# A row scale moved behind the first expert: router and gather read the residual without its norm

## The reference, cut to what matters

```
h = x * rsqrt(mean(x*x) + EPS) * g_ffn            # RMSNorm; the first factor is one number per row
logits = h @ w_router                             # 256 x 8
top_v, top_i = top_k(logits, 2); wts = softmax(top_v)
x = x + sum_e combine[:, e] * (silu(h @ w1[e]) * (h @ w3[e])) @ w2[e]
out = rmsnorm(x, g_final)
```

## Time and profile before

| | |
|---|---|
| median of three runs | 1710.83 us (1710.59 to 1711.66) |
| the profiled execution | 1712.28 us, span 1710.5 us |
| TensorE busy, share of the span | 1668.2 us, 98% |
| VectorE busy | 1283.9 us, 75% |
| ScalarE busy | 1051.2 us, 61% |
| mean granted clock of TensorE | 0.995 |
| DMA | 493.96 MB, mean 289 GB/s |

### The profile page before, as it was taken

The page is one execution under the profiler, slowest core; times in us unless marked ns, Lnnn a source line. Parts: engine busy times, 40 slices in busy tenths (PEclk is TensorE's granted clock), DMA queues, the critical chain, the costliest instruction groups (busy, mean ns, idle before and its releaser), DMA issues.

```text
span 1710.5 us, 24615 instructions
## 1 busy us (share of the span) xinstructions
PE 1668.2 (98%) x9340; PEld 1449.8 (85%) x9340; DVE 1283.9 (75%) x1221; ACT 1051.2 (61%) x965; POOL 18.3 (1%) x44
## 2 busy tenths in 40 slices
PE   7999999999999999999999999999999999999996
PEld 6989998999988999888888888888888888888885
DVE  6655575655565556678888888888888888888996
ACT  5534544433453454457777777777777777777774
POOL 1000000000000000000000000000000000000100
PEclk9999999999999999999999999999999999999998
DMA  8633449885473335769999999999999999999992
GB/s 277 199 123 100 123 148 354 302 262 177 157 219 125 123 115 170 260 244 385 354 388 390 357 387 390 355 397 385 364 393 377 364 392 362 386 391 358 393 394 110
DMA packets 252569, 493.96 MB, mean 289 GB/s; under 512 B 8310, under 2 KB 86720, under 8 KB 252496
## 3 DMA queue, kind: packets, MB, share of 16 engines
q1 hardware_dynamic: 247424, 479.23, 78.3%
q10 hardware_dynamic: 3664, 9.44, 1.4%
q0 software_dynamic: 1408, 4.28, 0.7%
HBM read 473.52 MB, written 19.40 MB: 288 GB/s over the span
## 4 chain that ended last, share of the span: by engine, by line
PE 95%; DVE 2%; issue 1%; ACT 1%; DMA 0%; DVEq 0%; ACTq 0%; SPq 0%
PE bank L601 34%; PE bank L975 24%; PE bank L1007 18%; PE bank L979 12%; PE bank L591 3%; PE bank L992 1%; PE bank L825 1%; PE bank L796 1%; PE bank L639 1%; DVE wlo L1567 0%; PE bank L778 0%; PE bank L1019 0%; PE bank L651 0%; DMA hn<-in_mem 0%; ACT pbuf L1232 0%
## 5 line engine op out<-in xcount | busy, mean ns | idle before, releaser
L1924 DVE TENSOR_TENSOR wlo<-raw,whi 128x2048 fp32r<-128x2048 f32 x328 | 748.1, 2288 | 108.9 <-ACT whi L1432 108.7
L1432 ACT ACTIVATE whi<-raw 128x2048 fp32r<-128x2048 f32 x328 | 627.8, 1919 | 179.5 <-PE bank L979 94.2
L1567 DVE TENSOR_TENSOR wlo<-raw,whi 128x2048 fp32r<-128x2048 f32 (+3 forms) x113 | 249.3, 2210 | 196.7 <-ACT whi L1219 196.5
L975 PE MATMUL bank<-whi,yT_hi 128*128 128x512 f32 x896 | 354.3, 395 | 0.8 <-issue 0.8
L975 PE MATMUL bank<-whi,yT_lo 128*128 128x512 f32 x896 | 349.3, 390 | 0.0
L1219 ACT ACTIVATE whi<-raw 128x2048 fp32r<-128x2048 f32 (+3 forms) x113 | 209.0, 1851 | 131.9 <-PE bank L601 114.1
L601 PE MATMUL bank<-hT_hi,whi 128*128 128x256 f32 x848 | 243.7, 287 | 3.1 <-DVE hT_lo L1589 1.8
L979 PE MATMUL bank<-wlo,yT_hi 128*128 128x512 f32 x896 | 240.0, 390 | 0.0
L601 PE MATMUL bank<-hT_hi,wlo 128*128 128x256 f32 x848 | 239.9, 283 | 0.0
L601 PE MATMUL bank<-hT_lo,whi 128*128 128x256 f32 x848 | 239.8, 283 | 0.0
L979 PEld LDWEIGHTS bank<-wlo,yT_hi 128*128 128x128 f32 x896 | 168.2, 188 | 35.6
(11 more groups left out here) (263 smaller groups left out, 1788.7 us busy)
## 6 DMA issues: line engine op xcount, KB each, us to landing
raw<-in_moe_w SPq DMA_DIRECT2D x336, 1024.0 KB, 7.5
raw<-in_w_in SPq DMA_DIRECT2D x36, 1024.0 KB, 5.3
raw<-in_dense_w SPq DMA_DIRECT2D x30, 1024.0 KB, 8.0
raw<-in_w_br SPq DMA_DIRECT2D x12, 1024.0 KB, 5.1
raw<-in_w_mkv SPq DMA_DIRECT2D x8, 1024.0 KB, 6.4
raw<-in_w_out SPq DMA_DIRECT2D x8, 1024.0 KB, 5.0
rows_by_slot<-qxT SPq DMA_DIRECT2D x15, 512.0 KB, 8.8
y_by_slot<-qxT SPq DMA_DIRECT2D x9, 512.0 KB, 8.4
```

Of the source, the lines that this page charges most:

```text
L975: nc.tensor.matmul(b[:, :], hselT[a][:, half, tok(k)], w[:, k, :], start=(half + k + a == 0), stop=False)
L1432: nc.scalar.activation(whi[:, (E0 + n) % SPLIT, :], raw[:, n % RAW, :], ACT.Copy).then_inc(hi_ready, 1)
L1567: V.tensor_tensor(wlo[:, m % SPLIT, 0:size], raw[:, pieces[n][1], 0:size], whi[:, m % SPLIT, 0:size].bitcast(F32), ALU.subtract).then_inc( ...
L1924: V.tensor_tensor(wlo[:, s, :], raw[:, n % RAW, :], whi[:, s, :].bitcast(F32), ALU.subtract).then_inc(lo_ready, 1)
```

## The change

The router's product and expert 0's gather read x itself, times g_ffn but without the row scale.

- The transposes read `x_sb`. Their first half (`transpose_residual(0)`) stands in TensorE's queue before w_out's last piece, the second (`transpose_residual(1)`) and a `keep_clock` of 4 between the two halves of the router's product. The high and low parts of the transposed rows move accordingly on ScalarE and VectorE: half of them, and the split of the router's weights, come before the last two updates of x. The bursts of 20 and 10 identity matmuls before the transposes and the router are gone.
- `normalise` is replaced by the row scales alone, copied to `r_tok`. The difference of the two largest logits is multiplied by it before the exponential.
- The split rows `hn_part` are gone. `gather` multiplies `x_sb` by `sel` in full fp32, 16 matmuls instead of 32. Two further matmuls gather the row scales of expert 0's slots into `r_slot` ([128, 1]).
- VectorE makes expert 0's low parts right after `sel`, then `r_slot`, then the slots, and last `rows_out`, which before was made ahead of the logits.
- `e_silu` applies `r_slot` as its scale, and `hidden` multiplies e3 by it, in every block of every expert. In each turn of the loop VectorE writes ones into `r_slot` ahead of expert j + 1's block 0, and ScalarE (before its silu) and VectorE (before `hidden`) wait for that on the semaphore `unit_scale`.
- Some PSUM banks are assigned anew.

```diff
@@ PSUM plan
-            take(("logT", l), bank=6)
-            take(("logits", l), bank=7)
-            take(("rank", l), bank=6)
+            take(("logT", l), bank=4)
+            take(("logits", l), bank=5)
+            take(("rank", l), bank=4)
             take(("rows0", l, 0), bank=7)
             take(("rows0", l, 1), bank=6)
+            take(("rslot", l), bank=3)
@@ tensor
+            def transpose_residual(half):
+
+                for n in (2 * half, 2 * half + 1):
+                    b = claim(("nT", 3 * DEPTH - 1, n))
+                    for t in range(T):
+                        read(pe, ("out", DEPTH - 1, t, half))
+                        for c in range(2):
+                            a = c * SEQ + t * P
+                            ins = nc.tensor.transpose(b[:, a:a + P], x_sb[:, t, tok(2 * n + c)], ident[:, :])
+                    mark(ins, ("nT", 3 * DEPTH - 1, n))
...
+                        if l == DEPTH - 1 and n * k:
+                            transpose_residual(0)
                         w = weight(("out", l, n, k), KD // 2)
...
-            keep_clock(("logT", l), 10)
-            mark(acc3(b[:, 0:SEQ], lambda a, k: router[a][:, k, :], lambda a, k: hT[a][:, k, :], range(KD),
-                      True, True, 3 * l + 2), ("logT", l))
+            for half in range(2):
+                if half:
+                    transpose_residual(1)
+                    keep_clock(("logits", l), 4)
+                ins = acc3(b[:, 0:SEQ], lambda a, k: router[a][:, k, :], lambda a, k: hT[a][:, k, :],
+                           range(4 * half, 4 * half + 4), half == 0, half == 1, 3 * l + 2)
+            mark(ins, ("logT", l))
...
-                        for a in range(2):
-                            ins = nc.tensor.matmul(b[:, c * CAP:(c + 1) * CAP], hn_part[a][:, t, tok(4 * n + c)],
-                                                   sel[:, t, :], start=(t + a == 0), stop=(t + a == T))
+                        ins = nc.tensor.matmul(b[:, c * CAP:(c + 1) * CAP], x_sb[:, t, tok(4 * n + c)],
+                                               sel[:, t, :].bitcast(F32), start=(t == 0), stop=(t == T - 1))
...
+            pe.wait_ge(scale_ready, 1)
+            b = claim(("rslot", l))
+            for t in range(T):
+                ins = nc.tensor.matmul(b[:, 0:1], sel[:, t, :].bitcast(F32), r_tok[:, t:t + 1],
+                                       start=(t == 0), stop=(t == T - 1))
+            mark(ins, ("rslot", l))
@@ scalar
+                        if l == DEPTH - 1:
+                            act.wait_ge(router_in, 16)
+                            nc.scalar.activation(router[0][:, :, 0:NE], wrt[:, :, :], ACT.Copy).then_inc(router_hi, 1)
+                            hi_parts(room(("nT", 3 * l + 2, 0)))
+                            norm_hi(3 * l + 2, hT, c_of["ffn"] + l * KD, (0, 1))
                 if l == DEPTH - 1:
-                    act.wait_ge(router_in, 16)
-                    nc.scalar.activation(router[0][:, :, 0:NE], wrt[:, :, :], ACT.Copy).then_inc(router_hi, 1)
+                    norm_hi(3 * l + 2, hT, c_of["ffn"] + l * KD, (2, 3))
...
-            for t in range(T):
-                nc.scalar.activation(hn_part[0][:, t, :], hn[:, t, :], ACT.Copy).then_inc(hn_hi, 1)
...
-                free(nc.scalar.activation(silu_m, b[:, :], ACT.Silu), (phase, "e1", b_))
+                free(nc.scalar.activation(silu_m, b[:, :], ACT.Silu, scale=r_slot[:, 0:1]), (phase, "e1", b_))
...
                 e_hi("loop", e_room("loop", "e1", 0), j)
+                act.wait_ge(unit_scale, j + 1)
                 e_silu("loop", 0, j)
@@ vector
+                        if l == DEPTH - 1:
+                            dve.wait_ge(router_hi, 1)
+                            V.tensor_tensor(router[1][:, :, 0:NE], wrt[:, :, :], router[0][:, :, 0:NE].bitcast(F32),
+                                            ALU.subtract).then_inc(router_lo, 1)
+                            lo_parts(room(("nT", 3 * l + 2, 0)))
+                            norm_lo(3 * l + 2, hT, c_of["ffn"] + l * KD, (0, 1))
+                            lo_parts(room(("out", l, 0, 1)))
-                normalise(3 * l + 2)
                 if l == DEPTH - 1:
...
+                    norm_lo(3 * l + 2, hT, c_of["ffn"] + l * KD, (2, 3))
+                    row_scales(3 * l + 2)
+                    V.tensor_copy(r_tok[:, :], rin[:, 6:8]).then_inc(scale_ready, 1)
+                else:
+                    normalise(3 * l + 2)
...
-            V.tensor_tensor(gap[:, 0, :], top_v[:, :, 1], top_v[:, :, 0], ALU.subtract).then_inc(gap_ready, 1)
+            link(V.tensor_tensor(gap[:, 0, :], top_v[:, :, 1], top_v[:, :, 0], ALU.subtract))
+            V.tensor_tensor(gap[:, 0, :], gap[:, 0, :], r_tok[:, :], ALU.mult).then_inc(gap_ready, 1)
...
+            b = full(dve, ("rslot", l))
+            free(V.tensor_copy(r_slot[:, :], b[:, 0:1]), ("rslot", l))
+            read(dve, ("rslot", l))
...
-                free(V.tensor_tensor(g32_m, silu_m, b[:, :], ALU.mult), (phase, "e3", b_))
+                free(V.scalar_tensor_tensor(out=g32_m, in0=b[:, :], scalar=r_slot[:, 0:1], in1=silu_m, op0=ALU.mult,
+                                            op1=ALU.mult), (phase, "e3", b_))
...
                 e_lo("loop", e_room("loop", "e1", 0), j)
+                read(dve, ("loop", "e3", NM - 1), j)
+                V.tensor_copy(r_slot[:, :], ones[:, 0:1]).then_inc(unit_scale, 1)
                 hidden_lo("loop", NM - 1, j)
                 e_lo("loop", e_room("loop", "e3", 0), j)
+                dve.wait_ge(unit_scale, j + 1)
                 hidden("loop", 0, j)
```

More of the change, by code:

```diff
@@ L273, in build @@
         cur = sb("cur", [P, 2, T])
+        r_tok = sb("r_tok", [P, T])
+        r_slot = sb("r_slot", [P, 1])
         place = sb("place", [P, T, NE])
@@ L381, in build @@
         rows_scaled = sem("rows_scaled")
+        scale_ready = sem("scale_ready")
+        unit_scale = sem("unit_scale")
         slots_known = sem("slots_known")
@@ L387, in build @@
         ey_hi = sem("ey_hi")
-        hn_hi = sem("hn_hi")
-        hn_lo = sem("hn_lo")
         cur_ready = sem("cur_ready")
@@ L1237, in half_square, with norm_hi @@
                 square(x_sb[:, t, n * HALF:(n + 1) * HALF], HALF, 6 + 2 * t + n)
-            def norm_hi(i, dst, gain):
-                for n in range(4):
+            def norm_hi(i, dst, gain, parts=range(4)):
+                for n in parts:
                     b = full(act, ("nT", i, n))
@@ L1477, in _ @@
             hi_parts(room(("head", "e1", 0)))
+            read(act, ("rslot", DEPTH - 1))
             e_silu("head", 0, 0)
@@ L1580, in normalise_memory, with norm_lo @@
                     V.tensor_scalar(hn[:, t, :], hn[:, t, :], rin[:, 8 + t:9 + t], None, ALU.mult).then_inc(hn_ready, 1)
-            def norm_lo(i, dst, gain):
-                for n in range(4):
+            def norm_lo(i, dst, gain, parts=range(4)):
+                for n in parts:
                     b = full(dve, ("nT", i, n))
@@ L1844, in _ @@
                         free(V.tensor_tensor(part[1], g, part[0].bitcast(F32), ALU.subtract), ("up", l, c))
-            for t in range(T):
-                dve.wait_ge(hn_hi, t + 1)
-                V.tensor_tensor(hn_part[1][:, t, :], hn[:, t, :], hn_part[0][:, t, :].bitcast(F32),
-                                ALU.subtract).then_inc(hn_lo, 1)
-            dve.wait_ge(gain_row_in, 16)
-            for t in range(T):
-                V.scalar_tensor_tensor(out=rows_out[:, t, :], in0=x_sb[:, t, :], scalar=rin[:, 6 + t:7 + t],
-                                       in1=gain_row, op0=ALU.mult, op1=ALU.mult).then_inc(rows_scaled, 1)
             l = DEPTH - 1
@@ L1891, in _ @@
             select()
+            gain = c_of["ffn"] + (DEPTH - 1) * KD
+            for n in range(2):
+                b = full(dve, ("rows0", l, n))
+                dve.wait_ge(rows_hi, n + 1)
+                for c in range(4):
+                    part = [v[:, n, c * CAP:(c + 1) * CAP] for v in hselT]
+                    ins = V.scalar_tensor_tensor(out=part[1], in0=b[:, c * CAP:(c + 1) * CAP],
+                                                 scalar=cols[:, gain + 4 * n + c:gain + 4 * n + c + 1],
+                                                 in1=part[0].bitcast(F32), op0=ALU.mult, op1=ALU.subtract)
+                free(ins, ("rows0", l, n))
+            b = full(dve, ("rslot", l))
+            free(V.tensor_copy(r_slot[:, :], b[:, 0:1]), ("rslot", l))
+            read(dve, ("rslot", l))
             over = place[:, :, :]
@@ L1902, in _ @@
             V.tensor_scalar(more[:, :], most[:, 0:1], float(CAP), None, ALU.is_gt).then_inc(flag_ready, 1)
-            gain = c_of["ffn"] + (DEPTH - 1) * KD
-            for n in range(2):
-                b = full(dve, ("rows0", l, n))
-                dve.wait_ge(rows_hi, n + 1)
-                for c in range(4):
-                    part = [v[:, n, c * CAP:(c + 1) * CAP] for v in hselT]
```

(8 more changed lines are left out.)

16 lines of the change are left out of this document (6 added, 10 removed).

## The result

The changed kernel takes 1728.7 us, the median of four runs (1727.96 to 1731.56), against 1710.71 (1709.48 to 1711.66), the median of four runs of the kernel before: ratio 1.0108 (in square brackets, here and below, its 95% interval: [1.0095, 1.012]), 1.1% slower. Predicted were 1718.9 and a range of 1713.6 to 1727: the sign was right, and the loss, 18.0 us for 8.1, was more than twice as large. The profiled execution took 1729.35.

The account below looks back on a forecast made before the run. TensorE was taken to bound the expert loop, with almost no idle time. Terms -4.8 ahead of the experts, +12.3 for loop stalls and +0.6 for silu sum to +8.1 us: 1718.9 us, range 1713.6 to 1727.

Parts of the forecast that it names:

- Ahead of the experts, -4.8: Around the router: its output copied 7.2 us earlier, filler passes then cold; 4.8 us gained, bounds 1.7 to 7.0.
- The delay that I carried over from the earlier trace: TensorE near the router: 2.4 GHz returns 9.2 us after work stopped, as before, so near 727.1.
- The gather, zero: Expert 0's gather: 32 reduced-format passes become 16 full matmuls of two passes each; no cost, 0.3 in the bound.
- the rival of the double price: Expert 0's gather: four passes per full fp32 matmul would cost 3.5 us more, 1722.4 us in all; chance 2%.
- The stall at the loop's edge, 1.75 a turn: Loop turn's end: silu waits for VectorE's ones, so w2 starts 1.65 us late, restarting 0.1 slower; 12.3 over seven turns.
- 0.6 in all: Block 1 of each loop turn: silu's scale from a pointer takes 0.08 us longer and delays w2; range 0 to 1.2.
- the case without cover: Loop's other blocks: without the 0.25 us of room, silu's extra 0.08 counts 49 times, 3.9 us.
- Hidden, with some 5 us left for landing: Dispatch: GpSimd's four indirect DMAs, issued later, still land before ScalarE asks for their rows; zero cost, up to 2.
- The hidden wait: Rival, loop: silu's wait for the ones costs nothing, leaving the gain, 1706.6 us; chance 12%.
- The clock rival: Rival, loop: the stalls also lower TensorE's clock, 11.9 us more if in all seven turns, 1730.8 us; chance 12%.
- That the gain doesn't come: Rival, ahead of the loop: VectorE's queue gets longer than counted, so no gain, 1723.7 us; chance 5%.
- That the dispatch is late: Rival, dispatch to expert 1's rows: up to 2 us more, 1720.9 us; chance 4%.

Follow-up runs that it names:

- e7: Changed kernel with expert 0's row scale put into the gather's matrix, r_slot, pointers and unit_scale removed, row products and slots early: 1705.93 us.
- e2: Changed kernel with the copy of ones into r_slot put ahead of the low parts in VectorE's queue, right behind hidden of block 6: 1716.15 us.
- e3: Kernel before with the loop part alone: silu and hidden read r_slot (always ones), with the copy of ones and waits on unit_scale: 1727.19 us.
- e4: Kernel before with the chain of slots and the two row products behind expert 0's low parts, as in the change: 1720.55 us.
- e5: As e2, but silu and hidden don't read r_slot; copies and waits stay, expert 0's row scale is left out: 1712.83 us.
- e9: As e8, but with the low part of expert piece 2 behind the low parts of expert 0's rows: 1702.93 us.
- e10: Changed kernel with the two row products alone moved into VectorE's idle time ahead of the rank's result; slots stay late: 1723.28 us.
- e8: As e7, with piece 2's low part moved into VectorE's wait for the ranks, and the row products behind the slots: 1702.36 us.

## Why the prediction was wrong

By the trace: -5.7 ahead of the experts, +7.2 in expert 0, +15.3 in seven turns (2.19 each), in all +16.8 of the span's 17.1; 0.15 more is a longer wait in the last expert (2.56 us for the 2.41 of the earlier trace rows). I had -4.8, 0 and +12.9. Of the 9.0 us that the forecast of the span missed, 7.2 are the dispatch, 2.4 the loop, and -0.9 the larger gain.

- **Ahead of the experts, -4.8: right.** The copy was predicted at 721.6 and came at 721.44; the filler burst ran cold as said, and was shorter (4.50 for 5.2), since full speed came back at 725.7 and not at 727.1. Gain 5.7 (5.4 without the 0.3 that was there before), inside the bounds. The delay that I carried over from the earlier trace rows was the weak number. The Trainium skill (TensorE: Matmul & The Clock Gate, Part 1) has the switch vary from run to run; the runs agree: the same 24 fillers behind the same 3.98 us of idle time took 4.57 here and 5.49 in e7.
- **The gather, zero: right.** 3.59 for 3.52 us; the rival of the double price is refuted here. Its estimate took each of the four passes to be as long as a row's. The Trainium skill (FP8 and Floating Point Precision, TensorE Precision Notes) counts four passes for true FP32; the trace has two rows for each of the 16 matmuls, together no longer than two of the reduced format.
- **The stall at the loop's edge, 1.75 a turn: right.** TensorE idle for 1.54 to 1.59 plus a slower first matmul; e2 takes off 1.67 a turn. e3 shows it, as large, in a kernel with the old router.
- **"0.6 in all" for silu's longer pointer form: mis-sized.** Silu takes 0.69 us instead of 0.60. "In the other blocks some 0.25 us of room covers it" failed: in blocks 2 to 5 and at the turn's end the room was about nothing, and in block 1 nothing was lost. It costs 0.46 a turn, 3.2 in all (3.3 by the medians), near the 3.9 that I had given for the case without cover. The multiply in `hidden`, "free" in the prediction, takes 0.07 us more, which VectorE's idle time covers.
- **"Hidden, with some 5 us left for landing": the step that failed.** I counted on the old scale, the issues from 745.8 to about 751 and ScalarE's request at 756.60. By the spacing before (3.90 us from the first start, 736.13, to the last, 740.03) the last issue would start near 749.7, 6.9 us ahead of the request. On that scale (the rows after, plus the 5.7 us of gain) it started at 752.7, 3.0 late: 0.4 because the first started later, 2.6 because two of the three issues ahead of it took 2.23 and 2.40 us and not 0.95 to 1.06. And it landed at 761.1, 8.4 us after its start and not 6.9. Those 3.0 and 1.5 make the 4.5 us by which the rows missed the request. No row of mine showed a landing time; "5 us left" was a remainder, not a price. The miss itself I priced at "up to 2 more" ("if the DMAs meet the weights", which they did: the DMA share is 1.03 from 747 to 755.4), while TensorE paid all of it and then 2.4 us of low clock.
- **The rivals.** The hidden wait is refuted (seven stalls). The clock rival was right in kind and in the wrong place: seven stalls of 1.5 to 1.6 us left it at 1.00, one of 4.86 lowered it. That the gain doesn't come is refuted (5.4). That the dispatch is late was the rival that came true, given 4%, with under a third of its price.

Both prices of the failed step, that of a slow issue and that of the landing, stood in the trace of the kernel before, though not for these four: at its end GpSimd issues four other indirect DMAs (L1200, which fetch the experts' results), two of them beside a low part. They take 2.61 and 2.47 us, and the medians from issue to landing are 9.9 us for the first two and 9.3 for the others. The second, with the low part (VectorE, GpSimd):

```profile
1595.11 2.28 DVE L1924 TENSOR_TENSOR wlo<-raw,whi 128x2048 fp32r<-128x2048 f32 x1
```

```profile
1595.77 2.47 POOL L1200 DMA_INDIRECT hn<-y_by_slot,slot_i  x1 [0.31 <-issue]
```

Open is what sets the landing time. It was 8.4 to 9.3 us in the kernel after and 8.6 to 9.8 in e4, with the weights' DMAs issued from 741.91 on (747.43 in e4); the DMA share here was 0.50 up to 744, 0.87 up to 747, and 1.03 behind. No run took these loads away. For why an issue takes long beside a low part, see the last section. Open is also why the profiled runs fall into two groups, 1.5 us apart, ahead of every edit.

## What to carry to other kernels

Set a cover against the whole way of a transfer: the wait for its data, every issue beside what the other engines do then, the queues at that time, and the landing, each from a row. What is left over is not a price. A small write that another engine waits for belongs ahead of the long operations in its queue (one line moved gave back 12 us here). A scale that only one user needs belongs where that user's data is made, in `sel` once, and not on a path that all users walk.

## What the runs showed of the hardware

**Indirect DMAs of GpSimd beside VectorE's low parts.** The twelve traces hold 96 issues of indirect DMAs, eight in each. 42 began while VectorE ran a weights' low part (128x2048): 15 of the dispatch (three each in the kernel after, e2 and e5, four in e4, one each in e9 and e10) and 27 of those at the kernel's end. Each of the 42 ends 0.80 to 0.94 us after the end of that low part: in the kernel after, 741.75 and 742.68; in e10, 741.21 and 742.04; in e4, 747.26 and 748.20. So they took 1.49 to 3.08 us. The other 54 took 0.93 to 1.06, with VectorE idle, on its short chains or on the low parts of expert 0's rows, and also where a weights' low part began just behind them (e10, 738.72, low part 738.92: 0.97). An issue that had waited then ran beside the next low part without making it longer (743.55, two in 4.49 us). The Trainium skill (SBUF — State Buffer, Who interferes with whom) says that a VectorE instruction with two SBUF inputs contends with a GpSimd one that reads SBUF, and that whichever starts first holds the ports; a low part has two such inputs, and the issue reads `slot_i`. The 42 agree. The same section infers that such an instruction (`tensor_tensor`) does not hold up the making of a DMA's descriptors; the 42 speak against that. That the later low part wasn't held up doesn't follow from its rule either. No run changed the low parts' form, so this is a reading of times, not an experiment.

**The clock.** TensorE's clock fell after idle times of 3.98 and 4.86 us here and 7.76 in e4; it stayed at 1.00 after 1.78 (e8) and after the seven of 1.54 to 1.59, as it had after the 1.77 of the earlier trace rows and not after the 2.41 of the earlier trace rows.
